# A ring of weight buffers: a quarter of two experts' matrices per position in place of half of one

## What is computed

```python
for e in range(N_EXPERTS):
    a = jax.nn.silu(ht @ w_expert_gate[e]) * (ht @ w_expert_up[e])
    out = out + combine[:, e:e + 1] * (a @ w_expert_down[e]).astype(jnp.float32)
```

## Time and profile before

| | before |
|---|---|
| median of 3 runs | 812.87 us |
| the profiled execution's own time | 813.58 us |
| its span | 811.8 us |
| PE busy | 776.9 us (96%) |
| moved by DMA | 268.03 MB, mean 330 GB/s |
| DMA packets | 75270 |

### The profile page before, as it was taken

One profiled execution on the slowest core, in us unless ns is written; L12 is line 12 of the kernel. 1 busy time (PEld: TensorE's weight loads), 2 busy tenths in 40 slices (PEclk: granted clock), 3 DMA queues, 4 the chain that ended last, 5 costly groups with the idle time before them and its releaser, 6 DMA issues.

```text
span 811.8 us, 10142 instructions
## 1 busy us (share of the span) xinstructions
PE 776.9 (96%) x4170; PEld 447.5 (55%) x4170; DVE 236.1 (29%) x533; ACT 176.7 (22%) x321; POOL 103.0 (13%) x132
## 2 busy tenths in 40 slices
PE   8999999999999999999999999999998998999995
PEld 7888887888888888853333333333332332343332
DVE  4199869492551222531100111011101101101111
ACT  3104333657445000321111101100110010011001
POOL 5200064524200000001101000001000000000004
PEclk9999999999999999999999999999999999999998
DMA  9845587677849963599999999999999999999992
GB/s 328 239 141 192 162 244 217 174 212 195 260 139 385 401 249 146 195 346 429 422 427 397 424 428 424 428 427 424 429 423 430 428 425 426 422 428 422 419 417 82
DMA packets 75270, 268.03 MB, mean 330 GB/s; under 512 B 5710, under 2 KB 37562, under 8 KB 58447
## 3 DMA queue, kind: packets, MB, share of 16 engines
q1 hardware_dynamic: 73378, 264.26, 84.0%
q0 software_dynamic: 528, 1.90, 0.6%
q10 hardware_dynamic: 1317, 1.19, 0.5%
HBM read 259.26 MB, written 8.55 MB: 330 GB/s over the span
## 4 chain that ended last, share of the span: by engine, by line
PE 72%; DMA 14%; SPq 7%; DVE 2%; issue 2%; POOL 1%; ACT 1%; DVEq 0%; POOLq 0%
PE bank L1602 23%; PE bank L1979 19%; PE bank L2017 8%; SPq L537 7%; PE bank L1875 7%; DMA slot<-in_w_expert_gate_dram 5%; DMA slots<-in_w_expert_gate_dram 5%; PE bank L2026 4%; DMA early<-in_norm_final_g_dram 3%; PE bank L1822 2%; DMA slots<-in_w_in_dram 1%; PE bank L1712 1%; PE bank L1943 1%; PE bank L1634 1%; PE bank L2006 1%
## 5 line engine op out<-in xcount | busy, mean ns | idle before, releaser
L1602 PE MATMUL bank<-hT,slots 128*128 128x264 f32 x832 | 189.6, 388 | 0.0
L1979 PE MATMUL bank<-slots,hT 128*64 128x512 f32 x624 | 180.0, 601 | 5.8 <-DMA slots<-in_w_expert_gate_dram 4.1
L1602 PEld LDWEIGHTS bank<-hT,slots 128*128 128x128 f32 x832 | 156.8, 190 | 26.6 <-issue 0.6
L1460 DVE TENSOR_TENSOR early<-early,bank 128x512 f32<-128x512 f32 x16 | 11.0, 687 | 383.4 <-PE bank L1979 383.4
L1979 PEld LDWEIGHTS bank<-slots,hT 128*64 128x64 f32 x624 | 55.2, 138 | 101.4 <-issue 90.7
L2017 PE MATMUL bank<-slots,wrep 128*64 128x512 f32 x304 | 85.7, 595 | 4.2 <-ACT wrep L1028 4.0
L1979 PE MATMUL bank<-slot,hT 128*64 128x512 f32 x208 | 82.8, 594 | 1.6 <-DMA slot<-in_w_expert_gate_dram 1.6
L761 POOL COPY hT<-early 128x512 f32 x30 | 17.5, 612 | 375.4 <-PE bank L1979 290.2
L2026 PE MATMUL bank<-hT,diag 128*128 128x512 f32 x128 | 59.2, 605 | 0.2 <-ACT hT L1040 0.2
L2017 PEld LDWEIGHTS bank<-slots,wrep 128*64 128x64 f32 x304 | 26.9, 137 | 42.4 <-issue 35.3
L1200 DVE SCALAR_TENSOR_TENSOR slot<-slot,rows_buf 128x256 f32<-128x256 f32 x120 | 49.4, 487 | 0.0
(11 more groups left out here) (315 smaller groups left out, 827.0 us busy)
## 6 DMA issues: line engine op xcount, KB each, us to landing
slots<-in_w_expert_down_dram SPq DMA_DIRECT2D x17, 2048.0 KB, 32.3
slots<-in_w_expert_gate_dram SPq DMA_DIRECT2D x15, 2048.0 KB, 27.0
slots<-in_w_expert_up_dram SPq DMA_DIRECT2D x15, 2048.0 KB, 32.0
slots<-in_w_in_dram SPq DMA_DIRECT2D x13, 2048.0 KB, 9.9
slots<-in_w_expert_gate_dram SPq DMA_DIRECT2D x10, 1024.0 KB, 27.3
slot<-in_w_expert_gate_dram SPq DMA_DIRECT2D x5, 2048.0 KB, 31.5
slot<-in_w_expert_up_dram SPq DMA_DIRECT2D x5, 2048.0 KB, 27.5
slot<-in_w_expert_down_dram SPq DMA_DIRECT2D x5, 2048.0 KB, 37.3
```

Source lines behind the costliest of these rows:

```text
L1460: dve.tensor_tensor(act.rearrange("s (f c) -> s f c", f=FT), act.rearrange("s (f c) -> s f c", f=FT), bank[UP][:, :].rearrange("s (c f) -> ...
L1602: last = mm(out, w[:, a, t * P:(t + 1) * P], (hT if c else xgain)[:, a, :], start=(a == 0), stop=(a == KT - 1))
L1979: last = mm(out[sl, :], xe[:, a, sl], expert_view(p, kind, e, a // 4)[:, a % 4, :], start=(a == 0), stop=(a == KT - 1))
```

## The change

Pairs 0 and 15 (the outer two) are now filled by quarters: position j of a matrix kind holds quarter j of both experts' matrices, in one transfer of 1 MB whose runs are 4 KB (two per partition, one for each expert). `by_halves` now holds for pair 14 and for pair 1's down only. All three counts go up four times a pair, after each quarter of a gate, an up or a down, and every wait on them is scaled to suit (one of the seven of the other engines is shown in the diff). A position that was loaded by quarters is given back after its quarter; the others are given back after the same half as before.

```diff
+        def by_quarters(p):
+            return p in (0, PAIRS - 1)
+
         def by_halves(p, kind):
-            return p >= PAIRS - 2 or p == 0
+            return p == PAIRS - 2 or (p, kind) == (1, 2)
...
         def by_slot(i):
-            return not by_halves(i // 12, i % 12 // 4) and i % NR < NR - SINGLES
-
-        def expert_wait(pe, p, kind, e, h):
-
-            i = load_at(p, kind, e, h)
-            if by_slot(i):
-                i -= i % 2
+            p, kind = i // 12, i % 12 // 4
+            return not by_quarters(p) and not by_halves(p, kind) and i % NR < NR - SINGLES
+
+        def expert_wait(pe, p, kind, e, j):
+
+            if by_quarters(p):
+                if e:
+                    return
+                i = 12 * p + 4 * kind + j
+            else:
+                if j % 2:
+                    return
+                i = load_at(p, kind, e, j // 2)
+                if by_slot(i):
+                    i -= i % 2
             pe.wait_ge(ew_in[i % NR], 16 * loads_to(i))
...
                 if i >= NR:
                     p, kind, _, h = what(i - NR)
-                    sp.wait_ge((m_gate, m_up, m_down)[kind], 2 * p + h + 1)
+                    last = i % 4 if by_quarters(p) else 2 * h + 1
+                    sp.wait_ge((m_gate, m_up, m_down)[kind], 4 * p + last + 1)
 
             def load_half(i):
                 p, kind, e, h = what(i)
                 reclaim(i)
-                sp.dma_start(half_flat(i), expert_rows(kind, 2 * p + e)[:, h * HALF:(h + 1) * HALF]).then_inc(ew_in[i % NR], 16)
+                if by_quarters(p):
+                    both = (wg, wu, wd)[kind][2 * p:2 * p + 2].rearrange("e (p a) n -> p e (a n)", p=P)
+                    sp.dma_start(half_flat(i).rearrange("p (e c) -> p e c", e=2),
+                                 both[:, :, i % 4 * HALF // 2:(i % 4 + 1) * HALF // 2]).then_inc(ew_in[i % NR], 16)
+                else:
+                    sp.dma_start(half_flat(i), expert_rows(kind, 2 * p + e)[:, h * HALF:(h + 1) * HALF]).then_inc(ew_in[i % NR], 16)
...
-                se.wait_ge(m_gate, 2 * p + 2)
+                se.wait_ge(m_gate, 4 * p + 4)
...
                     for e in range(2):
-                        if a % 4 == 0:
-                            expert_wait(pe, p, kind, e, a // 4)
-                            if p == 0 and kind == 0:
-                                pe.wait_ge(first_xe, 2 * (a // 4) + e + 1)
+                        if a % 2 == 0:
+                            expert_wait(pe, p, kind, e, a // 2)
+                        if a % 4 == 0 and p == 0 and kind == 0:
+                            pe.wait_ge(first_xe, 2 * (a // 4) + e + 1)
...
-                    if a % 4 == 3:
+                    if a % 2 == 1:
                         last.then_inc(done, 1)
...
-                    if f % 2 == 1:
-                        last.then_inc(m_down, 1)
+                    last.then_inc(m_down, 1)
```

More of the change, by code:

```diff
@@ L418, in loads_to, with expert_view @@
             return sum(1 for j in range(i % NR, i + 1, NR) if j % 2 == 0 or not by_slot(j))
-        def expert_view(p, kind, e, h):
-            return half_flat(load_at(p, kind, e, h)).rearrange("p (a n) -> p a n", a=(FT if kind == 2 else KT) // 2)
+        def expert_view(p, kind, e, j):
+            if by_quarters(p):
+                part = half_flat(12 * p + 4 * kind + j)[:, e * HALF // 2:(e + 1) * HALF // 2]
+            else:
+                part = half_flat(load_at(p, kind, e, j // 2))[:, j % 2 * HALF // 2:(j % 2 + 1) * HALF // 2]
+            return part.rearrange("p (a n) -> p a n", a=(FT if kind == 2 else KT) // 4)
         def expert_src(kind, e):
@@ L758, in _ @@
                 pool.wait_ge(m_xall, 2 * BLOCK_OF[p] + 2)
-                pool.wait_ge(m_up, 2 * p)
+                pool.wait_ge(m_up, 4 * p)
                 for e in range(2):
@@ L1026, in pair @@
                 if p:
-                    se.wait_ge(m_down, 2 * p)
+                    se.wait_ge(m_down, 4 * p)
                 se.copy(actT, bank[4][:, :].rearrange("p (f s) -> p f s", f=FT)).then_inc(m_actT, 1)
@@ L1031, in pair @@
                 if p < PAIRS - 1:
-                    se.wait_ge(m_down, 2 * p + 2)
+                    se.wait_ge(m_down, 4 * p + 4)
                 else:
@@ L1458, in swiglu @@
                 dve.wait_ge(m_silu, p + 1)
-                dve.wait_ge(m_up, 2 * p + 2)
+                dve.wait_ge(m_up, 4 * p + 4)
                 dve.tensor_tensor(act.rearrange("s (f c) -> s f c", f=FT), act.rearrange("s (f c) -> s f c", f=FT),
@@ L1486, in _ @@
                 weigh(p)
-            dve.wait_ge(m_down, 2 * PAIRS)
+            dve.wait_ge(m_down, 4 * PAIRS)
             dve.tensor_copy(ytok[:, CHUNK:], bank[5][:, :]).then_inc(y_half, 1)
@@ L1973, in hidden @@
                     for e in range(2):
-                        if a % 4 == 0:
-                            expert_wait(pe, p, kind, e, a // 4)
-                            if p == 0 and kind == 0:
-                                pe.wait_ge(first_xe, 2 * (a // 4) + e + 1)
+                        if a % 2 == 0:
+                            expert_wait(pe, p, kind, e, a // 2)
+                        if a % 4 == 0 and p == 0 and kind == 0:
+                            pe.wait_ge(first_xe, 2 * (a // 4) + e + 1)
                         sl = slice(e * SLOTS, (e + 1) * SLOTS)
-                        last = mm(out[sl, :], xe[:, a, sl], expert_view(p, kind, e, a // 4)[:, a % 4, :],
+                        last = mm(out[sl, :], xe[:, a, sl], expert_view(p, kind, e, a // 2)[:, a % 2, :],
                                   start=(a == 0), stop=(a == KT - 1))
-                    if a % 4 == 3:
+                    if a % 2 == 1:
                         last.then_inc(done, 1)
@@ L2013, in down @@
                         for e in range(2):
-                            if f % 2 == 0 and i == 0:
-                                expert_wait(pe, p, 2, e, f // 2)
+                            if i == 0:
+                                expert_wait(pe, p, 2, e, f)
                             sl = slice(e * SLOTS, (e + 1) * SLOTS)
                             last = mm(bank[4 + i][sl, :], actT[:, f, sl],
-                                      expert_view(p, 2, e, f // 2)[:, f % 2, 512 * i:512 * i + 512],
+                                      expert_view(p, 2, e, f)[:, 0, 512 * i:512 * i + 512],
                                       start=(f == 0), stop=(f == FT - 1))
```

## The result

The changed kernel takes 813.04 us in the median of 19 runs, the kernel before 810.92 us in 19 runs. The ratio is 1.0020 with a 95% interval of 1.0013 to 1.0026: slower by 1.6 us (1.1 to 2.1). (The two medians alone lie 2.1 us apart; every comparison here goes by the ratio.) The forecast was +1.0 us, "the same" by its bound of 0.3%, and 813.9 us. "No change" lies outside the interval; the loss is on the side of the forecast's sum, and under that bound.

A forecast was written before the change was run, and what follows sets the result against it. Transfers bound the expert part, with a fixed GpSimd and VectorE tail behind the last byte. Terms 0 + 0.85 + 0.14 + 0 + 0 = +1.0 us on the 812.87 median gave 813.9 us; range 811.3 to 816.0, the forecast's own 812.5 to 815.

The forecast's parts named there:

- the same: Whole kernel: time within about 0.3%, 2.4 us, of no change; chance 0.78.
- The bound: Expert part, 360 to 790 us: transfers never pause at 424 GB/s, so bytes set the length; norm_final_g and GpSimd close it.
- Earlier return at the start: Pair 0's positions return earlier, but SP waits for the routing until 353.70 and the queue is full: 0 us.
- the 354 named as a sign of being wrong: Start of the stream: the prediction is wrong if the stream starts earlier than 354 us.
- The hole of 62 GB/s: Transfers from 352 to 354 us drop to 62 GB/s, which was put down to SP's wait for the routing.
- the 138 GB/s: Rate of the stretch with norm_final_g's copy, taken as the rate when a single row is read by all partitions.
- the shortfall behind the hole: Transfers from 354 to 360 us fall 456 KB short, at most 1.07 us; put down to the routing table's copy.
- Shorter runs: Pair 15's 12 loads in 4 KB packets at a full queue: 409 GB/s, 30.74 us in place of 29.89, +0.85 us.
- The rival of clashing reads: Pair 15's quarter loads clash in HBM: 391 GB/s or less, +2.3 us or more, 61 us at 138 GB/s; chance 0.13.
- Pair 1's down: Its runs go from 16 KB to 8 KB, 4.19 MB at 421 in place of 427 GB/s: +0.14 us.
- The end: PE ends its last down about 2.4 us earlier behind its last load, but GpSimd is busy with norm_final_g: 0 us.
- Counts and waits: Twice as many increments and PE's added wait in gate 15 cost nothing: 0 us.

The follow-up runs named there:

- pair 0 alone: Quarters in pair 0 only, halves in pair 15 and pair 1's down, against the kernel before: ratio 0.9997, -0.2 us.
- the norm early: norm_final_g's load issued before pair 13's loads, not behind pair 15's: ratio 1.0003 in the kernel before, 0.9990 in the changed kernel, both against the kernel before.
- the crossed kernel: Kernel before, but pair 15's rows land in the ring as two separated 4 KB pieces, still read by halves: ratio 1.0013, +1.1 us.
- pair 15 alone: Quarters in pair 15 only, pair 0 by halves and pair 1's down by expert, against the kernel before: ratio 1.0015, +1.2 us.

## Why the prediction was right

**The bound.** Right: the middle of the stream is at 426 GB/s in both kernels, and the chain's end is the same.

**Earlier return at the start, 0.** Right in effect: pair 0 alone is at -0.2 us, and load 20 went out 0.86 us behind load 17, as before. (It went out at 353.05, earlier than the 354 named as a sign of being wrong, but only because the mixer had ended earlier.) That SP could not use the return is right too; load 20 went out 1.7 us before load 17 once it was put ahead of the wait for the routing. Two readings behind this term were wrong. The hole of 62 GB/s does not belong to that wait: it is there with load 20 issued into it. And the 138 GB/s is not the price of a copy of one row to all partitions: the engines are busy at 0.33 there, and in the kernel before with the norm early, which has no such copy at the end, 790 to 795 us is at 146 GB/s with a share of 0.35. That looks like the queue running out, and the rival's 61 us, priced by it, have no ground. What the shortfall behind the hole is due to stays open; putting it down to the table's copy is not shown.

**Shorter runs, +0.85.** The term that made the result, and the step with the best witness. The line through the 2 KB and 8 KB rows gave 409 GB/s for 4 KB; 408 and 409 were measured in every kernel with all of pair 15 in 4 KB packets. The Trainium skill ("DMA: Bandwidth & Descriptors", section "iDMA fabric — 4 AXI ports for 8 engines, asymmetric across TPBs") gives 408.7 GB/s for one load stream from SP with 4 KiB rows, and these rates agree. The rival of clashing reads fell: the crossed kernel, without any such reads, has the same rate. The Trainium skill's warning of power-of-two pitches (the same page, section "Latency and other measured facts") is for pitches from 512 KiB up, and no run here has one; at a pitch of 16 KB no loss of that kind is left over.

**Pair 1's down, +0.14.** Too small to be seen: pair 0's kernel, which has it too, is at -0.2 with an interval of 1.5 us.

**The end, 0.** Right: PE finishes its part earlier, as forecast, and GpSimd's norm_final_g covers it. The early norm shows the cover by taking it away. What the forecast left out is that the cover lies over two tiles, and the second has 0.9 us of slack, so in the kernel before less than 1.6 us was to be had.

**Counts and waits, 0.** Not contradicted: the kernel with quarters in pair 0 only counts four times in every pair, and it is at -0.2.

**The sum.** +1.0 against +1.6 (1.1 to 2.1). The two halves of the change, run apart, add up to +1.0 (-0.2 and +1.2). Whether 0.6 us more belongs to a term that I sized too small or to the scatter of the runs stays open: the interval of pair 15 alone, 0.5 to 1.9, holds both. The traces do not help: from load 17 to the landing of norm_final_g they show 0.4 us on the average of three against three. So the sign, the place and the rate are shown, the size only to within a factor of about two. That the absolute 813.9 came within 0.9 us of 813.04 is in part luck: it started from a median of three that stood 2 us above the nineteen, and the loss was 0.6 larger than forecast.

## What to carry to other kernels

Where transfers are the bound from start to end, finer buffers do not make the stream shorter; they make its packets shorter, and those are paid for. What finer grain can gain lies at the two ends, and only if nothing else waits there: look for the last transfer in the queue and for the wait in which the issuing queue sits before you split a load. Here a small load that was queued last hid what the split gained at the end, and moving it cost nothing that could be measured; at the start no gain is shown. And before you compare a stretch in two executions, start it from the same event in both.

## What the runs showed of the hardware that was not expected

Two 4 KB runs that adjoin on both sides were moved as 8 KB packets (75270 packets, none added), while the same runs apart in the ring gave 1536 more and 409 GB/s in place of 419 to 421. Whether the program or the chip joins them no trace here tells.

A queue of shorter packets is shorter in time: norm_final_g took 24.72 us from issue to landing behind 8 KB packets and 17.06 us behind 4 KB ones (24.8 and 25.4 in two other kernels with 8 KB, 16.8 to 17.1 in four with 4 KB). The transfers did not run dry before it in either case.

Loads that are issued need not flow: in the three us behind the issue of load 19 every trace moves 45 to 119 GB/s, with one more load of 1 MB issued in them or not.

The packet's price at a full queue stayed one line over the lengths seen: 388 and 383 GB/s with 2 KB runs (kernel before and after), 408 to 409 with 4 KB, 419 to 421 with 8 KB.
